# Output projection of a hybrid decoder step in token rows, with w_out kept on chip and the samples' attention between its tiles

## The reference, cut to what matters

```python
o_att = _rmsnorm(attend(q, k, v), g_subln) * (1.0 - lam_init)
mix = jnp.concatenate([o_att.reshape(b, t, D_ATT), y_lru], axis=-1)
mix = jnp.einsum('bte,ed->btd', mix, w_out)
x = x + gt_m * _rmsnorm(mix, g_post_mix)
h = _rmsnorm(x, g_pre_ffn) * (1.0 + sc_f) + sh_f
gate, up = jnp.split(jnp.einsum('btd,df->btf', h, w_ffn_in), 2, axis=-1)
f = jnp.einsum('btf,fd->btd', jax.nn.silu(gate) * up, w_ffn_out)
```

## Time and profile before

| | us |
|---|---|
| median of 3 runs (3102.24 to 3107.18) | 3106.33 |
| the profiled execution, its own time | 3107.55 |
| its span in the trace | 3105.6 |
| PE busy, share of the span | 87% |
| DVE, ACT, POOL | 54%, 34%, 29% |
| mean granted PE clock, share of 2.4 GHz | 0.94 |

### The profile page before, as it was taken

The page is one execution under the profiler, slowest core; times in us unless marked ns, Lnnn a source line. Parts: engine busy times, 40 slices in busy tenths (PEclk is TensorE's granted clock), DMA queues, the critical chain, the costliest instruction groups (busy, mean ns, idle before and its releaser), DMA issues.

```text
span 3105.6 us, 42942 instructions
## 1 busy us (share of the span) xinstructions
PE 2698.7 (87%) x16348; PEld 2536.4 (82%) x16348; DVE 1692.5 (54%) x2477; ACT 1051.6 (34%) x1608; POOL 912.2 (29%) x399
## 2 busy tenths in 40 slices
PE   5999998588889557864599999999978999999994
PEld 2999998477677417764499999999978999999993
DVE  2689776677667442677344444444475444444446
ACT  3545553377777403544211111111231111111111
POOL 2566655223232105443222222222141212222212
PEclk8999999799999768987799999999999999999997
DMA  5345443433332335644411111111132111111122
GB/s 216 118 146 189 151 135 125 119 92 86 85 105 64 113 144 208 213 159 166 151 58 41 41 61 41 41 41 61 41 127 81 59 41 41 61 41 41 41 73 56
DMA packets 162785, 300.54 MB, mean 97 GB/s; under 512 B 14730, under 2 KB 128042, under 8 KB 156530
## 3 DMA queue, kind: packets, MB, share of 16 engines
q1 hardware_dynamic: 152034, 282.25, 27.3%
q10 hardware_dynamic: 10640, 16.77, 1.7%
HBM read 252.63 MB, written 46.39 MB: 96 GB/s over the span
## 4 chain that ended last, share of the span: by engine, by line
PE 45%; DVE 3%; DMA 2%; ACT 1%; POOL 0%; issue 0%; DVEq 0%; ACTq 0%; POOLq 0%
PE p_y L1962 16%; PE p_g L1946 15%; PE p_u L1946 15%; DMA p_stage<-h 1%; DVE p_y L2144 1%; DVE p_xin L2156 1%; DVE p_h_lo L2133 1%; ACT p_h_hi L2050 0%; DVE p_rstd L2141 0%; POOL p_stage L1906 0%; DVE p_y L2127 0%; DMA yT<-p_xin 0%; DVE p_f_lo L2115 0%; DMA p_xin<-x 0%; ACT p_stage L2059 0%
## 5 line engine op out<-in xcount | busy, mean ns | idle before, releaser
L2127 DVE TENSOR_TENSOR p_y<-p_y 128x342 f32<-128x342 f32 (+1 forms) x1008 | 483.8, 511 | 730.6 <-PE p_y L1962 730.5
L1946 PE MATMUL p_g<-p_h_hi,p_w_hi 128*128 128x342 f32 (+1 forms) x1056 | 340.7, 323 | 34.6 <-DVE p_h_lo L2133 34.6
L1962 PE MATMUL p_y<-p_f_hi,p_w_hi 128*128 128x342 f32 (+1 forms) x1056 | 344.5, 326 | 28.5 <-DVE p_y L2125 15.6
L328 POOL TENSOR_TENSOR p_w_lo<-p_wraw,p_w_hi 128x1024 fp32r<-128x1024 f32 x100 | 294.3, 2954 | 214.0 <-ACT p_w_hi L389 213.8
L1899 POOL TENSOR_TENSOR p_w_lo<-ffn_wraw,p_w_hi 128x1024 fp32r<-128x1024 f32 x66 | 160.3, 2429 | 642.6 <-ACT p_w_hi L2027 642.6
L1962 PE MATMUL p_y<-p_f_hi,p_w_lo 128*128 128x342 f32 (+1 forms) x1056 | 342.1, 324 | 0.0
L1962 PE MATMUL p_y<-p_f_lo,p_w_hi 128*128 128x342 f32 (+1 forms) x1056 | 341.5, 323 | 0.0
L1946 PE MATMUL p_g<-p_h_lo,p_w_hi 128*128 128x342 f32 (+1 forms) x1056 | 339.4, 321 | 0.0
L1946 PE MATMUL p_g<-p_h_hi,p_w_lo 128*128 128x342 f32 (+1 forms) x1056 | 338.6, 321 | 0.0
L1946 PE MATMUL p_u<-p_h_lo,p_w_hi 128*128 128x342 f32 (+1 forms) x1056 | 338.3, 320 | 0.0
L1946 PE MATMUL p_u<-p_h_hi,p_w_hi 128*128 128x342 f32 (+1 forms) x1056 | 337.4, 319 | 0.0
(11 more groups left out here) (260 smaller groups left out, 5812.0 us busy)
## 6 DMA issues: line engine op xcount, KB each, us to landing
p_wraw<-w_in SPq DMA_DIRECT2D x100, 512.0 KB, 4.8
ffn_wraw<-w_ffn SPq DMA_DIRECT2D x22, 1536.0 KB, 6.5
p_wraw<-w_ffn SPq DMA_DIRECT2D x22, 1536.0 KB, 6.5
p_wraw<-w_out SPq DMA_DIRECT2D x48, 512.0 KB, 6.8
p_ada<-w_ada SPq DMA_DIRECT2D x32, 512.0 KB, 4.5
z<-p_zout SPq DMA_DIRECT2D x48, 206.0 KB, 2.8
p_ada_ring<-w_ada SPq DMA_DIRECT2D x4, 2048.0 KB, 20.8
ps_keys<-cache_k SPq DMA_DIRECT2D x32, 256.0 KB, 8.6
```

Of the source, the lines that this page charges most:

```text
L328: pool.tensor_tensor(w_lo[s][:], wraw[:, s, :], w_hi[s][:].bitcast(F32), ALU.subtract).then_inc(lo_done, 1)
L1946: mm = pe.matmul(bk[par][:, 0:W], a[s][:, KT * half + k, :], b[:, k, c0:c0 + W], start=r == 0, stop=r == 3 * KT - 1)
L1962: mm = pe.matmul(yb[q % YB][:, 0:W], a[s][:, 2 * KT + m, :], b[:, c0:c0 + W], start=r == 0, stop=r == 2)
L2127: dve.tensor_tensor(y[:, m, c0:c0 + W], y[:, m, c0:c0 + W], yb[q % YB][:, 0:W], ALU.add).then_inc(yadd, 1)
```

## The change

`sample_attention` is no block of its own any more, and `output_projection` is written anew. It works in token rows: a tile has 128 tokens on the partitions and all 1024 features as columns in two PSUM banks (`OP`), 16 tiles of 128 and one of the 8 samples (`NTL` = 17). The mix is now the stationary operand and w_out the moving one, 512 columns at a time, so w_out is loaded and split once (8 loads; hi on ACT, lo on DVE for even and POOL for odd k) and stays in `w_hi`, `w_lo`. The gate, which is one value per feature, is spread to rows `gg` at the start (ones x diagonal, L1514) and for the samples turned (L1520). Sums of squares come from ACT's `accum_out`. The results x1 and the normed x are turned back to feature rows on PE (`turn_x`, `turn_h`, 8 transposes each per tile), copied by DVE (x1T) or scaled and shifted by ACT (h2), and stored per tile. The steps are staggered: in step s PE does tile s and turns tile s - 2; DVE and ACT do gate, residual and norms of tile s - 1. All loads but six small ones are on SP, in program order. The samples' attention is spread over the steps: keys x q of sample s - 1 on DVE in steps 1 to 8, scores turned in step 9, softmax in step 10, weights turned in step 11, value products behind tiles 11 and 12, now into four 32-row groups of the bank, sums in step 13, norm in step 14, and the result goes straight into tile 16's mix. In which steps values are loaded says `VLOADS`. w_ffn's first unit is loaded in step 8. The input gets x in token rows; `pick` is repeated four times.

```diff
-KR = 4
-def sample_attention(nc, mods, io):
+NTL = SEQ // P + 1
+VS = 6
+VLOADS = {2: (0, 1), 3: (4,), 4: (5,), 8: (2,), 9: (3,), 12: (6, 7)}
...
+            def turn_x(t, i):
+                n = height(t)
+                if i == 0:
+                    wait(pe, "x1", t + 1)
+                wait(pe, "h2", 2 * t - 1 + i)
+                for k in range(4):
+                    mm = pe.transpose(TB[i][:, k * P:k * P + n], x1[t % 2][0:n, (4 * i + k) * P:(4 * i + k + 1) * P],
+                                      mods["ident"][0:n, 0:n])
+                mm.then_inc(S["x_turned"], 1)
...
+            def main(t, k):
+                if k == 0:
+                    wait(pe, "m_lo", t + 1)
+                    wait(pe, "y1", t - 1)
+                    if t == 1:
+                        wait(pe, "ggs", 1)
+                if t == 0:
+                    wait(pe, f"w_lo{k}", 1)
+                r = height(t)
+                for n, (a, w) in enumerate(((m_hi, w_hi), (m_hi, w_lo), (m_lo, w_hi))):
+                    for c in (0, 512):
+                        mm = pe.matmul(OP[t % 2][0:r, c:c + 512], a[t % 2][:, k, 0:r], w[k][:, c:c + 512],
+                                       start=k == 0 and n == 0, stop=k == KT - 1 and n == 2)
...
+            def weigh(b):
+                if b == 0:
+                    wait(pe, "pT", 1)
+                pe.wait_ge(v_in[b % VS], 16 * NPG * (b // VS + 1))
+                for g in range(NPG):
+                    mm = pe.matmul(QA[32 * g:32 * g + 32, :], pT[:, g, b, :], vals(b)[:, g, :], start=b == 0,
+                                   stop=b == NS - 1)
+                mm.then_inc(S["values"], 1)
...
+            split_w(0)
+            split_m(0)
+            split_w(1)
+            wait(act, "mods", 1)
+            for k in range(KT):
+                if k >= 2:
+                    wait(act, f"spread{k - 2}", 1)
+                act.activation(diag[:, k % 2, :], mods["ident"][:], ACT.Copy, scale=mods["gate_m"][:, k, 0:1]
+                               ).then_inc(once(f"diag{k}"), 1)
+            split_w(2)
+            split_w(3)
+            wait(act, f"spread{KT - 1}", 1)
+            act.activation(gg[:], OP[1][:], ACT.Copy).then_inc(once("gg"), 1)
+            split_w(4)
+            split_w(5)
+            wait(act, "ggs_turned", 1)
+            act.activation(ggs[:], OP[1][0:NS, :], ACT.Copy).then_inc(once("ggs"), 1)
+            split_w(6)
+            split_w(7)
...
+            def residual(t):
...
+                dve.scalar_tensor_tensor(out=x1[t % 2][0:n, :], in0=OP[t % 2][0:n, :], scalar=rs[0:n, t, 0:1],
+                                         in1=g[0:n, :], op0=ALU.mult, op1=ALU.mult).then_inc(S["y1"], 1)
+                dve.wait_ge(x_in, 16 * (t + 1))
+                wait(dve, "y1", t + 1)
+                dve.tensor_tensor(x1[t % 2][0:n, :], x1[t % 2][0:n, :], x[0:n, :], ALU.add).then_inc(S["x1"], 1)
...
+            def read_x(t, i):
+                n = height(t)
+                if i == 0 and t:
+                    dve.wait_ge(x1_out, 16 * t)
+                wait(dve, "x_turned", 2 * t + i + 1)
...
-        "w_out": c(np.stack(tiles(f(i["w_out"])[0], range(KT)))),
+        "w_out": c(f(i["w_out"])[0].reshape(KT, P, D)),
...
-        sample_attention(nc, mods, io)
```

The order of the loads on SP, per step:

```diff
+            for s in range(END):
+                for b in VLOADS.get(s, ()):
+                    if b >= VS:
+                        load_vals(b)
+                if s + 2 < NTL:
+                    load_mix(s + 2)
+                if 0 < s < NTL:
+                    load_x(s)
+                if 0 <= s - 2 < NTL:
+                    store_x1(s - 2)
+                    store_h2(s - 2)
+                if 2 <= s + 1 < NS:
+                    load_keys(s + 1)
+                for b in VLOADS.get(s, ()):
+                    if b < VS:
+                        load_vals(b)
```

More of the change, by code:

```diff
@@ L1304, in sample_attention @@
-        DV = {n: i + 1 for i, n in enumerate(names_d)}
-        block = ctx.enter_context(nc.Block())
-        def load(e, cache, to, landed, b):
-            for g in range(NPG):
-                page = e.value_load(table[0:1, b * NPG + g:b * NPG + g + 1], min_val=0, max_val=POOL - 1)
-                e.dma_start(to[:, g, :], io[cache][bass.ds(page, 1)].rearrange("o p f -> (o p) f")
-                            ).then_inc(landed, 16)
+        osq = buf("osq", [P, BH])
+        rn = buf("rn", [P, BH])
@@ new lines, in output_projection, with vals @@
+        rows = buf("rows", [P, NH * P])
+        rowsel = pT[0:NS].rearrange("p g b n -> p (g b n)")
+        OP = [bank(f"out{i}", D) for i in range(2)]
+        TB = [bank(f"turn{i}") for i in range(2)]
+        QA, QB2 = bank("sa"), bank("sb")
+        def vals(b):
+            v = b % VS
+            if v < 2:
+                return wraw[:, 2 * v:2 * v + 2, :].rearrange("p a (g f) -> p (a g) f", g=2)
+            return keys[v - 2][:] if v < 4 else vmore[v - 4][:]
+        tab_in, z_in, con_in, x_in, x1_out, h2_out = (
+            sem("tab_in"), sem("z_in"), sem("con_in"), sem("x_in"), sem("x1_out"), sem("h2_out"))
@@ new lines, in output_projection @@
+        w_in = [sem(f"w_in{i}") for i in range(RW)]
+        mix_in = [sem(f"mix_in{i}") for i in range(2)]
+        k_in = [sem(f"k_in{i}") for i in range(2)]
+        v_in = [sem(f"v_in{i}") for i in range(VS)]
+        S = {n: sem(n) for n in (
+            "w_hi", "m_hi", "m_lo", "out", "xT", "h2", "qb", "values")}
+        CYCLES = {"act_tile": ("sq1", "root1", "sq2", "root2"),
+                  "dve_tile": ("inv1", "y1", "x1", "inv2", "xn"),
+                  "pe_tile": ("x_turned", "x_turned", "h_turned", "h_turned"),
+                  "pages": ("prod", "red")}
@@ new lines, in _ @@
+            sp.wait_ge(x1_out, 16 * NTL)
+            sp.wait_ge(h2_out, 16 * NTL)
+        @block.gpsimd
+        def _(pool):
+            pool.memset(self_w[:], 0.0).then_inc(once("self_zero"), 1)
+            for k in range(1, KT, 2):
+                wait(pool, "w_hi", k + 1)
+                pool.tensor_tensor(w_lo[k][:], wraw[:, k % RW, :], w_hi[k][:].bitcast(F32), ALU.subtract
+                                   ).then_inc(once(f"w_lo{k}"), 1)
+            wait(pool, "qb", NS)
+            pool.memset(pT[:], 0.0).then_inc(once("p_zero"), 1)
```

804 lines of the change are left out of this document (395 added, 409 removed).

## The result

| | before | after |
|---|---|---|
| median of 4 runs each, us | 3105.64 (3102.24 to 3107.18) | 2964.74 (2963.24 to 2967.05) |
| ratio, 95% interval | | 0.9548 [0.9532, 0.9565] |
| span of the profiled execution, us | 3105.6 | 2965.2 |
| mean granted PE clock | 0.94 | 0.96 |

The kernel is 140.9 us faster; 2967 was forecast, with a range of 2950 to 2998.

The account below looks back on a forecast made before the run. PE was taken to bound the new block. Its terms sum to 296.9 us instead of 436.4, 139.5 less: 2968.0 from the profiled 3107.55, and 2967 us for the median, which is 1.2 lower. Range 2950 to 2998.

Parts of the forecast that it names:

- start to the end of the first tile: Block start, covered by nothing: first matmul at 11 us, then gate rows and weight splits; 39.5 us, bounds 28 and 52.
- 16 tiles' matmuls: Projection after the first tile: 48 matmuls of 512 columns per tile, 11.1 us each, 178 us in all.
- six spreads: Samples' query spreads on PE, priced like the old value products at 0.95 us each: 5.7 us.
- value products: Samples' 32 value products in four 32-row groups, overlapping by a factor of 3.0: 10.2 us, bounds 7.6 and 30.4.
- seams: An allowance of 2 us in the block's sum, not explained further.
- tail: Behind the last tile: about 9 us of work plus waits for stores; 18.5 us against 48.7, bounds 12 and 30.
- Rival (1): Tiles 1 to 16: PE paces every step, 12.9 us each, 13.9 with keys; 2967 us; chance 0.66.
- Rival (2): Samples' value products on PE don't overlap: 30.4 us instead of 10.2, time 2987 us; chance 0.12.
- Key steps: Steps with keys, 13.9 us: DVE's 10.7 us of work ends near 13.2; mix and x arrive 2 to 5 us early.
- rival (3): DVE or SP paces steps with keys and pages, one late mix or x: 25 us in all, 2992; chance 0.15.
- Rival (4): SP's queue, every step: transfers pace the block; 3155 us without overlap, 3096 by the skill page; chance 0.03.
- The clock: PE's clock may stay low in the start's short bursts; from tile 1 on no gaps, so nothing more is costed.

Follow-up runs that it names:

- one-group run: All 32 value products go into one 32-row group of the bank instead of four, against the changed kernel; 2983.65 us, ratio 0.96.

## Why the prediction was right

By the terms of its sum, in us:

| term | forecast | measured |
|---|---|---|
| start to the end of the first tile | 39.5 | 37.6 |
| 16 tiles' matmuls | 178 | 174.7 |
| transposes, 15 tiles | 27 | 28.5 |
| six spreads | 5.7 | 7.6 |
| value products | 10.2 | 7.5 |
| small products | 3 | 3.2 |
| seams; in fact late mix and x | 2 | 4.3 |
| tail | 18.5 | 16.5 |
| into the FFN | 13.0 | 12.9 |
| sum | 296.9 | 292.6 |

The rounded terms add up to 292.8. The sum is off by 4.3 us while its terms are off by 16 taken together: those for the start, the tiles' matmuls, the products and the tail were too large, those for the transposes, the spreads and the seams too small. That the total came so near is in part luck; no seam was found, and the 2 us set aside for them met a loss of another kind.

*Rival (1), PE as the pace*, is what happened, and three runs show it: one tile costs what its matmuls cost, doubling DVE's reduction adds nothing, and 20.5 us more of products add 20.2. The forecast's reading of the earlier trace rows held: two 512-column matmuls start 0.455 us apart, so 48 take 10.9 (forecast 11.1). The turned groups cost 1.9 per tile (12.81 less 10.9), forecast 1.8.

*Value products.* The forecast took the factor of 3.0 from 16 records of 128 columns; with 512 columns it is 3.7 against the same kernel's one-group form, and the lower bound of 7.6 is what PE spends. A likely reason, not shown by a run: the row's 0.64 us holds a matmul's way through the array once, which weighs more on 16 short records; at the 7.6 / (64 x 512) = 0.23 ns measured here they would take 0.47 us, an estimate. Rival (2) would have been the one-group run: 2983.65 for 2987 forecast. The Trainium skill ("TensorE: Matmul & The Clock Gate", section Measured speedup vs the span model) gives 2.38 for three column tiles of this size; that is 0.79 per tile, where four give 0.92 here. By its figure the term would have been 12.8, an estimate; the measured 7.6 decides.

*Spreads* were undersized. PE's timeline at one of them:

```profile
1125.73 0.63 PE L1495 MATMUL p_out<-p_w_hi,p_m_lo 128*128 128x512 f32 x2
1126.29 1.12 PE L1529 MATMUL p_sa<-p_qrow,p_pT 8*128 8x512 f32 x2
1127.34 0.73 PE L1495 MATMUL p_out<-p_w_hi,p_m_hi 128*128 128x512 f32 x2
1127.91 0.62 PE L1495 MATMUL p_out<-p_w_lo,p_m_hi 128*128 128x512 f32 x2
```

The spread itself holds PE 1.05 us, but the f32r pair ahead of it takes 0.56 and the one behind it 0.57 instead of 0.455, so the step grows by 1.27. The forecast had that term for the turns and left it out here.

*Start.* The right length from a wrong chain. The forecast had the first matmul at 11 us and the gate rows behind it; what happened is that z held PE until 13.0 us and ACT with it, a link that the forecast did not have, though the order of instructions shows the turn at the head of PE's queue. It had allowed for later links more than they took: it priced the whole first tile at 1.2 GHz, and in the trace the granted clock is 0.99 from 1087.0 to 1093.5 us and again from 1097.2 to 1109.1, with 0.50 from 1094.2 to 1097.0 between them.

*Tail.* The waits that the forecast named are there, and shorter than its allowance (timeline of the tail):

```profile
1343.79 0.19 DVE L1740 COPY p_x1T<-p_turn 128x32 f32<-128x32 f32 x1 [2.35 <-DMA x<-p_x1T]
...
1347.47 0.28 ACT L1653 ACTIVATE p_h<-p_turn 128x32 f32<-128x32 f32 x2 [3.72 <-DMA h<-p_h]
...
1351.20 13.46 SPq L1920 DMA_DIRECT2D p_stage<-h  x2
```

*Key steps.* For DVE the forecast's 10.7 us of work was exact (14.08 less the 3.35 idle), but it put DVE's end at 13.2 of 13.9: it added a wait for the second turn that DVE hardly has. DVE ends 12.2 us into the step, 1.9 before its end, and then waits 1.5 more for ACT's root in the next one: that is the 3.35. What can be added without touching PE is thus more than the 0.7 us that the forecast saw, and the doubled reduction took 2.3 of it. For SP the count that mix and x "arrive 2 to 5 us ahead of need" failed: it priced pages at 1.09 us each and saw 13 us in step 2, but not that the steps behind it leave no time to catch up (4.87 + 3.63 + 0.43 + 0.58 + 0.88 + 2.85 = 13.2 us of issues from 1153.14 on, in SP's timeline). So the "one late mix or x" of rival (3) came true three times and cost 4.3 us. The late pages of samples 6 and 7 did cost nothing, as forecast.

*Rival (4)* stayed away: 278 to 310 GB/s with 512 KB tiles and 256 KB pages. The Trainium skill's rule on batch size ("DMA: Bandwidth & Descriptors", section Measured, at least 1 MiB for 75% of the peak) is not borne out for a stream of transfers: 256 KB pages alone moved 389 GB/s in the kernel before, 0.89 of the 436 GB/s that the page takes as the peak. In the new block, with transfers a quarter and half of 1 MiB, the 278 to 310 GB/s are 0.64 to 0.71 of it, below the page's share, but with ACT issuing the pages the DMA engines are busy 0.95 to 1.00 and PE never waits between tiles. What fell is the forecast's estimate of 3096 us, which added up the page's price of one transfer as if none overlapped.

*The clock* cost nothing from tile 1 on (1.00 in tiles 1 to 16), as forecast. In the first tile it was 0.75 over the stretch, a good part of which PE spent waiting for z.
